# An expert's down weights loaded as one 16 KB piece per partition, and gate and up weights read with a stride of four columns

## What is computed

```
def expert_step(acc, p):
    w1, w3, w2, ge = p                       # gate, up: (1024, 512); down: (512, 1024)
    hdn = jax.nn.silu(xf @ w1) * (xf @ w3)   # (N, 512)
    return acc + ge[:, None] * (hdn @ w2).astype(jnp.float32), None

acc, _ = lax.scan(expert_step, jnp.zeros((N, D), jnp.float32), (w_gate, w_up, w_down, gate.T))
```

## Time and profile before

| what | value |
|---|---|
| median of 3 runs | 739.13 us (738.1 to 740.24) |
| the profiled execution | 744.82 us |
| its span, first to last instruction | 743.0 us |
| PE busy | 604.1 us (81%) |
| moved by DMA | 269.13 MB |
| chain that ended last, share of DMA / PE / SP's queue | 43% / 40% / 10% |

### The profile page before, as it was taken

The page is one execution under the profiler, slowest core; times in us unless marked ns, Lnnn a source line. Parts: engine busy times, 40 slices in busy tenths (PEclk is TensorE's granted clock), DMA queues, the critical chain, the costliest instruction groups (busy, mean ns, idle before and its releaser), DMA issues.

```text
span 743.0 us, 13746 instructions
## 1 busy us (share of the span) xinstructions
PE 604.1 (81%) x6164; PEld 370.3 (50%) x6164; DVE 225.6 (30%) x550; ACT 84.0 (11%) x224; POOL 49.3 (7%) x58
## 2 busy tenths in 40 slices
PE   4899999979999998998757777678667676787673
PEld 3678777756574455554334443344334343344342
DVE  4249689862131363321111111111111111111113
ACT  2211233211101111000000000000000000000003
POOL 4106440111000000000000000000000000000000
PEclk9999999989999999999987889879888889789887
DMA  9957959986999465999999999999999999999982
GB/s 300 302 235 252 289 188 415 299 324 265 415 414 415 203 255 218 413 424 421 424 412 423 421 423 418 419 425 420 418 419 424 421 417 420 421 423 418 421 367 89
DMA packets 44538, 269.13 MB, mean 362 GB/s; under 512 B 5076, under 2 KB 5896, under 8 KB 33975
## 3 DMA queue, kind: packets, MB, share of 16 engines
q1 hardware_dynamic: 37760, 230.91, 78.3%
q0 software_dynamic: 3072, 35.19, 11.6%
q10 hardware_dynamic: 3647, 2.14, 1.0%
HBM read 265.99 MB, written 2.46 MB: 361 GB/s over the span
## 4 chain that ended last, share of the span: by engine, by line
DMA 43%; PE 40%; SPq 10%; DVE 4%; issue 2%; ACT 1%; ACTq 0%; DVEq 0%
DMA ring<-w_up 37%; PE bank L1322 9%; SPq L476 8%; PE bank L1405 8%; PE bank L1543 4%; PE bank L1558 4%; PE bank L1497 4%; DMA front<-q_scratch 3%; DMA wf<-w_in 3%; PE bank L1474 2%; SPq L547 2%; DVE ring L998 1%; PE bank L1338 1%; PE bank L1305 1%; PE bank L1353 1%
## 5 line engine op out<-in xcount | busy, mean ns | idle before, releaser
L1322 PE MATMUL bank<-ring,front 128*32 128x256 f32 x2048 | 164.5, 491 | 106.5 <-DMA ring<-w_up 101.4
L1322 PEld LDWEIGHTS bank<-ring,front 128*32 128x32 f32 x2048 | 89.9, 140 | 173.3 <-issue 149.0
L1186 DVE COPY front<-bank 128x256 f32<-128x256 f32 x32 | 13.6, 425 | 247.3 <-PE bank L1322 247.3
L1338 PE MATMUL bank<-ring,front 128*32 128x256 f32 x1024 | 61.1, 379 | 0.7 <-DVE front L1191 0.7
L1497 PE MATMUL bank<-hT,ring 128*128 128x264 f32 x256 | 61.1, 396 | 0.4 <-ACT front L754 0.4
L1405 PE MATMUL bank<-hT,ring 128*128 128x264 f32 x256 | 59.9, 393 | 0.0
L1497 PEld LDWEIGHTS bank<-hT,ring 128*128 128x128 f32 x256 | 48.9, 195 | 10.4 <-issue 2.2
L1405 PEld LDWEIGHTS bank<-hT,ring 128*128 128x128 f32 x256 | 48.9, 193 | 9.4 <-issue 1.2
L1305 PE MATMUL bank<-front 128*32 128x256 f32 (+1 forms) x768 | 52.3, 385 | 0.3 <-DVE front L1097 0.3
L811 ACT ACTIVATE front<-bank 128x128 f32<-128x128 f32 x32 | 8.9, 277 | 385.3 <-PE bank L1330 385.3
L1338 PEld LDWEIGHTS bank<-ring,front 128*32 128x32 f32 x1024 | 33.3, 110 | 22.6 <-DVE front L1191 0.9
(11 more groups left out here) (293 smaller groups left out, 492.1 us busy)
## 6 DMA issues: line engine op xcount, KB each, us to landing
ring<-w_gate SPq DMA_DIRECT2D x31, 2048.0 KB, 34.1
ring<-w_down SPq DMA_DIRECT2D x31, 2048.0 KB, 34.4
ring<-w_up SPq DMA_DIRECT2D x31, 2048.0 KB, 30.6
ring<-w_in SPq DMA_DIRECT2D x8, 2048.0 KB, 25.0
ring<-w_out SPq DMA_DIRECT2D x2, 2048.0 KB, 16.6
front<-q_scratch SPq DMA_DIRECT2D x8, 256.0 KB, 5.3
ring<-w_up_pool SPq DMA_DIRECT2D x1, 2048.0 KB, 32.0
ring<-w_up_att SPq DMA_DIRECT2D x1, 2048.0 KB, 15.6
```

The source lines that it names most:

```text
L1322: last = m.matmul(bank[GATEUP][32 * g:32 * g + 32, 0:256], xgT[:, k % 2, k // 2], w[:, k, 256 * (g % 2):256 * (g % 2) + 256], start=k == 0 ...
L1338: last = m.matmul(bank[TDOWN][32 * g:32 * g + 32, 0:256], hE[:, j % 2, j // 2], wd[:, j, 256 * g:256 * g + 256], start=j == 0, stop=j == F ...
```

## The change

Down's source view becomes the same as that of gate and up: partition p takes rows 4p to 4p+3, one run of 16 KB. Block j of the down product then covers rows 4f+j, f being the partition. To match, output column c = 128 * (j % 2) + f of quarter g in the gate and up product must be hidden column 4f + j, so the moving operand is read with a step of four elements (16 bytes). The last expert's four down parts take row 4p+j for each partition p: still 4 KB each, now 16 KB apart in memory.

```
@@ load_matrix
             src = t[("w_gate", "w_up", "w_down")[m]][0, bass.ds(e, 1)]
-            if m < 2:
-                eng.dma_start(slot[q], src.rearrange("e (p k) f -> p (e k f)", p=P)).then_inc(s_slot[q], 16)
-            else:
-                eng.dma_start(slot[q].rearrange("p (j n) -> p j n", j=FC), src.rearrange("e (j p) n -> p (e j) n", p=P)).then_inc(s_slot[q], 16)
+            eng.dma_start(slot[q], src.rearrange("e (p k) f -> p (e k f)", p=P)).then_inc(s_slot[q], 16)
@@ sync, last expert
-            src = t["w_down"][0, LAST].rearrange("(j p) n -> p j n", p=P)
+            src = t["w_down"][0, LAST].rearrange("(p j) n -> p j n", p=P)
@@ gate_up
-                        w = slot[q + g // 2].rearrange("p (k n) -> p k n", k=DK)
-                        last = m.matmul(bank[GATEUP][32 * g:32 * g + 32, 0:256], xgT[:, k % 2, k // 2], w[:, k, 256 * (g % 2):256 * (g % 2) + 256],
+                        w = slot[q + g // 2].rearrange("p (k f j) -> p k j f", k=DK, j=FC)
+                        last = m.matmul(bank[GATEUP][32 * g:32 * g + 32, 0:256], xgT[:, k % 2, k // 2], w[:, k, 2 * (g % 2):2 * (g % 2) + 2],
                                         start=k == 0, stop=k == DK - 1)
```

## The result

The change makes the kernel slower by half a percent: 742.42 us median of 15 runs (740.43 to 748.44) against 738.74 us before (15 runs), ratio 1.005, 95% interval 1.0031 to 1.0069. The forecast was 731.2 us.

The account below looks back on a forecast made before the run. Weight loads, 6 MB per expert, were taken to set the pace, PE second some 5 us away. Down loads gain 8.0 us, the step and other parts nothing: 739.1 - 8.0 = 731.1, said as 731.2 us, range 727 to 740.

Parts of the forecast that it names:

- I take no cost, the value of the nearest row: Gate and up read with a 16-byte step: no cost, from stationary reads at L1383 and L1392; upper bound four times 3.66 us.
- rival 2: At L1322 the step makes gate_up slower than PE can hide: 793 us at three times, 896 at four; chance 0.12.
- rival 3: Step doubles gate_up, hidden in the steady part; ends cost 8.1 us against a gain of 8.0: 739 us; chance 0.08.
- The mis-sized term: Down loads of experts 3 to 30 in 16 KB packets: 28 loads, 0.284 us less each, 8.0 us in all.
- The price per load, 0.284 us: Saving per down load, 5.21 to 4.93 us, from mean window rates of 402 GB/s for down and 425 for gate and up.
- The check against 15.16 us: One expert's loads at window rates, 5.21 + 2 * 4.93 = 15.07 us, called close to 15.16 from PE's starts over 24 experts.
- The lower bound of 4.4 us: Smallest down-load gain by the extremes of the windows: 0.16 us a load, 411 against 424 GB/s.
- the spaced rows of the last down load: Last expert's four down parts, 4 KB packets 16 KB apart: costs nothing, at most 0.6 us.
- the fall of the packet count: Sign in the profile after: packets under 8 KB fall by 28 + 3 loads of 512, some 15,900.
- the dip: Slower down-load windows, 393 to 411 GB/s; forecast gone, all windows between 345 and 700 us at 424 GB/s or more.
- the 2.4 times of the prediction: In the steady part gate_up may grow by 5.0 us, to 2.4 times its length, before PE sets the pace.
- the zero for the down loads of experts 0 to 2: Cheaper down loads of experts 0 to 2, issued before 259 us, are hidden behind the routing: no gain.

Follow-up runs that it names:

- the probes: Kernel before plus ten PE probes after experts 2 to 11, reading an unchanged tile at steps 1 to 8 in one, two or four column groups; 740.32 us, one run.

## Why the prediction was wrong

**What bounds the kernel** was read rightly: the loads, with PE some 5 us behind, and 28 down loads on the path.

**The step that failed** is "I take no cost, the value of the nearest row", for gate and up read with a step of 16 bytes. The cost is 3.8 us for each `gate_up`, and some 8.1 us for the whole (742.42 - 734.32; each against the kernel before beside it, 3.7 + 4.6 = 8.3). Had the step cost nothing, the time would have lain in the range: the kernel without it took 734.32 us.

The row chosen could not bear it. It was a stationary read, 128 columns at a time, at the very start of the program, and its yardstick, the 330 ns of L1392, was itself unsteady. In six of the ten profiles of this case, that of the changed kernel among them, the same unstepped loads have a median of 188 ns, in the other four, that of before among them, 330 or 333, while the stepped ones of x stay at 226 to 231. Which of the two it is does not go with the step, and why it changes was not found.

```profile
L1380 PEld LDWEIGHTS bank<-cea,x x16: 185/226/226, 6.7 to 9.7; 128*128 128x128 f32 x16
...
L1389 PEld LDWEIGHTS bank<-front,ones x6: 181/188/192, 11.4 to 12.0; 128*128 128x128 f32 x4, 8*128 8x128 f32 x2
```

With these numbers of the changed kernel's profile the same comparison would have said that the step costs. The rule of the Trainium skill (Advanced Engine Details and Errata, "SBUF Cachelines") that was weighed against it in rival 2 held here, as the probes show (3.8 us with two hits on a line, 7.4 with one); rival 2 got a chance of 0.12 and rival 3, the doubling, 0.08.

**Rival 3 is what happened** on the side of the cost, and its working holds: `gate_up` doubled, hidden in the steady part, showing at the first slot and at the last halves, "8.1 in all". Measured: 8.1 between the medians of the changed kernel and the one without a step, 7.7 for the two end experts alone. That the first agrees to the tenth is luck: from the first `gate_up` the traces of the same two kernels differ by 463.7 - 454.1 = 9.6 us. What remained was its other side, set against a gain of 8.0 that was too large.

**The mis-sized term** is the down loads: 8.0 us expected, 4.6 measured (3.5 to 6.9), and 5.9 between the medians of the two kernels with the step. From the first `gate_up` the traces give 460.5 - 454.1 = 6.4 us without the step and 469.2 (751.6 - 282.41) - 463.7 = 5.5 with it. The price per load, 0.284 us, came from windows of 3.5 us. They read low for small pieces, 402 GB/s on average where the kernel with all weights in 4 KB pieces shows 409 over 355 us; why was not tested. The long windows give the price better: 3 * 2.097 MB at 421 and at 427 GB/s are 14.94 and 14.73 us, 0.21 us for a set and 28 * 0.21 = 5.9 us.

The check against 15.16 us in the prediction deceived, because 15.16 is an average over two kinds of interval between the starts of `gate_up`. Most are 14.8 to 15.0 us, and each seventh is 16.4 to 16.5, in before as in the kernel without a step (14.7 and 16.2). Before:

```profile
376.42 5.54 PE L1322 MATMUL bank<-ring,front 128*32 128x256 f32 x64 [5.69 <-DMA ring<-w_up]
391.38 6.58 PE L1322 MATMUL bank<-ring,front 128*32 128x256 f32 x64 [3.88 <-DMA ring<-w_up]
406.28 5.35 PE L1322 MATMUL bank<-ring,front 128*32 128x256 f32 x64 [2.77 <-DMA ring<-w_up]
```

and without the step:

```profile
282.58 3.66 PE L1319 MATMUL bank<-ring,front 128*32 128x256 f32 x64 [1.42 <-DVE front L1103]
...
359.19 6.01 PE L1319 MATMUL bank<-ring,front 128*32 128x256 f32 x64 [5.34 <-DMA ring<-w_up]
375.38 6.44 PE L1319 MATMUL bank<-ring,front 128*32 128x256 f32 x64 [4.65 <-DMA ring<-w_up]
390.06 5.35 PE L1319 MATMUL bank<-ring,front 128*32 128x256 f32 x64 [2.70 <-DMA ring<-w_up]
...
702.93 6.51 PE L1319 MATMUL bank<-ring,front 128*32 128x256 f32 x64 [3.82 <-DMA ring<-w_up]
```

From 376.42 to 406.28 it is 14.9 us an expert, below the 15.07 that the window rates give; held against that interval the check would have said that 402 GB/s is too low. What makes the seventh interval longer no run shows. The lower bound of 4.4 us stands just under the measured 4.6, and the interval reaches below it.

**Right:** the spaced rows of the last down load cost nothing (`down` of expert 31 starts 0.69 us after `turn_hidden`, released by DVE, in before, in the changed kernel and in the one without the step), the fall of the packet count, the dip gone (one window of the earlier trace rows at 421 GB/s, a little under the 424 that was forecast), and that a `gate_up` of twice its length, which is less than the 2.4 times of the prediction, is hidden in the steady part. The 2.4 itself was not tested, nor was the zero for the down loads of experts 0 to 2 by itself.

**Where the cost of the step lies** the traces show. From the first `gate_up` to that of expert 30 it is 425.4 us in the changed kernel (702.40 - 276.99) and 420.4 without the step (702.93 - 282.58), 5.1 us more; from there to the end 38.3 (740.7 - 702.40) and 33.8 (736.7 - 702.93), 4.5 more. Of the 5.1, 3.8 belong to the first slot, which `gate_up` of expert 0 frees that much later. One more is a gap in the queue. In the changed kernel the loads of expert 4 are issued 15.7 us after those of expert 3, at 300.21, and these need 14.7, so the rate falls just then (stretch, us, PEclk, DMA share, GB/s):

```profile
300.00:301.00 1.00, 1.00 0.77 328
301.00:302.00 1.00, 1.00 0.76 197
302.00:303.00 1.00, 1.00 0.85 311
```

Without the step they follow after 11.9 us, and the same three windows move 426, 442 and 426 GB/s. At 426 the changed kernel's three have lost 1.0 us. In the kernel with the step at both ends only, where expert 4's loads follow after 11.9 us too, 4.2 us come ahead of expert 30 and 2.7 behind it, against before. Of the 4.5 us at the end, 1.0 lies between the `gate_up` of expert 30 and that of 31 (716.02 - 702.40 against 715.55 - 702.93) and 3.5 behind it. Still open is why the medians have 8.1 in all and the traces, single executions, 9.6.

## What to carry to other kernels

A work item that is hidden in the middle of a long pipelined loop is not hidden in its first and last turn; price it there by itself, since two experts of 32 carried 7.7 of some 8 us. When one edit buys a cheaper load with a dearer read of an operand, look for the place where the new order can be made on the least data: here turning 256 columns once instead of reading them with a step 32 times gave the gain of 4.2 us without the loss. And where the trace has no row like the new access, a probe or a wide range belongs there, not the nearest row's zero. Before an average period is used as a check, look at the single intervals: here a few long ones hid that the price was a third too high.

## What the runs showed of the hardware

A float32 moving operand of 256 columns was read at full speed with a step of 1 or 2 elements (3.7 and 3.8 us for the 64 records), at two thirds of it with 3 (5.6) and at half with 4 or 8 (7.4 and 7.6). With all 128 columns of the array or with four groups of 32 it took the same. Whether a stationary operand pays for its step in the same way was not measured by itself: the turning with a step took 1.18 against 0.44 us, but in 16 records in place of two.

Weight loads in 4 KB packets moved 409 GB/s and in 16 KB packets 427, 4% apart, at DMA shares of 1.03 and 1.01.

With the longer matmuls the clock stayed up as well. From 345 to 700 us the granted clock of the changed kernel is 0.99, with idle times of 0.58 to 2.9 us ahead of `gate_up`, where it was 0.84 before, with idle times of 2.4 to 5.7 us and stretches at 1.2 GHz behind them. The pairs that differ by the step alone say the same: 0.85 without and 0.99 with it at 16 KB, 0.84 and 0.98 at 4 KB. So 3.8 us more at full clock cost the steady part less than it seems: before, `gate_up` took 5.2 to 6.6 us there in most experts, and now 7.5.

```profile
345.00:700.00 355.00, 327.07 (x3728) 0.99 1.01 426
```

That is the window of the changed kernel, with PE's busy time and records ahead of the clock. And this is before, around the `gate_up` that starts at 345.06 behind 2.41 us of idle time and takes 5.35:

```profile
344.50:346.00 1.50, 1.00 1.02 407
346.00:347.50 1.50, 0.55 1.10 442
347.50:349.00 1.50, 0.50 1.06 429
```
